# Two of eight K-tile pairs of ten up strips by Strassen's seven products, with the inner activations kept whole until the down stage

## What is computed

```python
def swiglu(x, w_up, w_down):
    g, u = jnp.split(x @ w_up, 2, axis=-1)      # w_up 2048 x 11264, w_down 5632 x 2048
    return (jax.nn.silu(g) * u) @ w_down

def reference(x, ...):
    h = x
    for l in range(DEPTH):                      # DEPTH = 1
        h = h + 0.5 * rms_norm(swiglu(rms_norm(h, ffn1_pre[l]), ffn1_up[l], ffn1_down[l]), ffn1_post[l])
        mix = hybrid_mixer(rms_norm(h, mix_pre[l]), ...)
        h = h + rms_norm(mix, mix_post[l])
        h = h + 0.5 * rms_norm(swiglu(rms_norm(h, ffn2_pre[l]), ffn2_up[l], ffn2_down[l]), ffn2_post[l])
    return h
```

## Time and profile before

| | |
|---|---|
| median of 3 runs | 2430.61 us (2430.49 to 2430.75) |
| profiled execution, its own time | 2430.32 us |
| its span in the trace | 2428.5 us |
| granted TensorE clock, mean | 0.999 |
| TensorE busy | 2412.1 us, 10823 matmuls |
| VectorE busy | 1293.1 us, 1395 instructions |
| ScalarE busy | 1155.4 us, 1340 instructions |
| GpSimd busy | 213.7 us, 400 instructions |
| up stages | 22 strips, 20 of them (2 to 11 of each block) touched by the change |

### The profile page before, as it was taken

The page is one execution under the profiler, slowest core; times in us unless marked ns, Lnnn a source line. Parts: engine busy times, 40 slices in busy tenths (PEclk is TensorE's granted clock), DMA queues, the critical chain, the costliest instruction groups (busy, mean ns, idle before and its releaser), DMA issues.

```text
span 2428.5 us, 32988 instructions
## 1 busy us (share of the span) xinstructions
PE 2412.1 (99%) x10823; PEld 1986.7 (82%) x10823; DVE 1293.1 (53%) x1395; ACT 1155.4 (48%) x1340; POOL 213.7 (9%) x400
## 2 busy tenths in 40 slices
PE   9999999999999999999999999999999999999998
PEld 7888888888887788887888888888888888888887
DVE  5555555554547555555545554555655555555444
ACT  6454544543445454454544444444554554544443
POOL 1212112110001000000000000000211212111000
PEclk9999999999999999999999999999999999999999
DMA  8767667665656555565656666655666666666664
GB/s 257 212 202 205 203 206 209 202 203 191 195 186 184 156 173 175 164 186 159 199 184 200 193 194 191 194 182 175 197 212 203 210 201 196 209 207 199 192 195 158
DMA packets 265725, 470.91 MB, mean 194 GB/s; under 512 B 21056, under 2 KB 54512, under 8 KB 265296
## 3 DMA queue, kind: packets, MB, share of 16 engines
q1 hardware_dynamic: 252752, 453.04, 60.5%
q0 software_dynamic: 12752, 17.24, 2.3%
q10 hardware_dynamic: 176, 0.07, 0.0%
HBM read 456.64 MB, written 2.10 MB: 189 GB/s over the span
## 4 chain that ended last, share of the span: by engine, by line
PE 98%; DVE 1%; ACT 1%; issue 0%; DMA 0%; ACTq 0%; DVEq 0%; SPq 0%; POOL 0%; POOLq 0%
PE acc L580 32%; PE acc L582 32%; PE acc L581 32%; PE bank L601 1%; PE bank L824 0%; PE bank L764 0%; PE bank L790 0%; DVE xT_lo L1232 0%; DVE w_lo L1221 0%; PE bank L845 0%; DVE h L1283 0%; ACT w_hi L923 0%; DMA h<-in_x_dram 0%; ACT xT_hi L945 0%; PE bank L811 0%
## 5 line engine op out<-in xcount | busy, mean ns | idle before, releaser
L1221 DVE TENSOR_TENSOR w_lo<-w_raw,w_hi 128x1024 fp32r<-128x1024 f32 x856 | 1048.3, 1227 | 1041.0 <-ACT w_hi L923 1033.1
L923 ACT ACTIVATE w_hi<-w_raw 128x1024 fp32r<-128x1024 f32 x856 | 906.3, 1061 | 1170.8 <-PE acc L582 1163.6
L580 PE MATMUL acc<-w_hi,xT_hi 128*128 128x512 f32 x2464 | 967.2, 393 | 6.1 <-DVE xT_lo L1232 3.9
L582 PE MATMUL acc<-w_hi,xT_lo 128*128 128x512 f32 x2464 | 959.9, 390 | 0.0
L581 PE MATMUL acc<-w_lo,xT_hi 128*128 128x512 f32 x2464 | 959.5, 389 | 0.0
L580 PEld LDWEIGHTS acc<-w_hi,xT_hi 128*128 128x128 f32 x2464 | 463.0, 188 | 105.6 <-issue 5.0
L582 PEld LDWEIGHTS acc<-w_hi,xT_lo 128*128 128x128 f32 x2464 | 462.8, 188 | 97.1
L581 PEld LDWEIGHTS acc<-w_lo,xT_hi 128*128 128x128 f32 x2464 | 463.1, 188 | 95.5 <-issue 1.0
L580 PE MATMUL acc<-w_hi,act_hi 128*128 128x512 f32 x704 | 273.9, 389 | 0.0
L582 PE MATMUL acc<-w_hi,act_lo 128*128 128x512 f32 x704 | 273.9, 389 | 0.0
L581 PE MATMUL acc<-w_lo,act_hi 128*128 128x512 f32 x704 | 273.9, 389 | 0.0
(11 more groups left out here) (145 smaller groups left out, 973.7 us busy)
## 6 DMA issues: line engine op xcount, KB each, us to landing
w_raw<-in_ffn_up_dram SPq DMA_DIRECT2D x352, 512.0 KB, 4.3
w_raw<-in_ffn_down_dram SPq DMA_DIRECT2D x176, 512.0 KB, 4.5
w_raw<-in_w_gate_dram SPq DMA_DIRECT2D x96, 512.0 KB, 4.1
w_raw<-in_w_in_dram SPq DMA_DIRECT2D x72, 512.0 KB, 3.6
w_raw<-in_w_in_dram SPq DMA_DIRECT2D x128, 256.0 KB, 3.0
w_raw<-in_w_ret_out_dram SPq DMA_DIRECT2D x32, 512.0 KB, 4.7
w_raw<-in_w_out_dram SPq DMA_DIRECT2D x32, 512.0 KB, 4.4
hid_T<-blocks POOLq DMA_DIRECT2D x352, 32.0 KB, 3.4
```

The lines of the kernel that those rows point to most:

```text
L580: pe.matmul(pair[m][:, :], xh, wh, start=(first and kk == 0), stop=False)
L582: mm = pe.matmul(pair[m][:, :], xl, wh, start=False, stop=(last and kk == KG - 1))
L923: act.activation(w_hi[:, s, :], w_raw[:, s, :], ACT.Copy).then_inc(w_rounded, 1)
L1221: dve.tensor_tensor(w_lo[:, s, :], w_raw[:, s, :], w_hi[:, s, :].bitcast(f32), ALU.subtract).then_inc(w_split, 1)
```

## The change

Strip 1 of each block stays as it was, in a section of its own (`first0`, `first1`) and no longer under Ifs; the loop runs over strips 2 to 11. There six of the eight K-tile pairs are multiplied as before, and pairs 6 and 7 each by Strassen's scheme in Winograd's form: the two K-tiles, the two row tiles and the gate and upper columns make a 2 by 2 by 2 block product of eight products, which becomes seven, of three matmuls each. Two products take plain blocks, one the input sum S4 with a weight block, three the sums S by T, and one a plain input with T4. They go into four scratch banks (`bank0` to `bank3`) and the accumulators, and VectorE puts them together (`u2` to `u5`) before Silu, which now reads SBUF. Row tile 1 has another RMS scale than row tile 0; `h_scaled` takes its input over to the scale of tile 0, and `to_tile1` takes the sums back.

Each pair needs four weight sums on VectorE (`t_raw`: one add over 1024 columns, two over 512), split like the weights (`t_hi`, `t_lo`). The upper group of such a pair is split only in its second half.

```diff
+QUADS = ((4, 5, 6), (10, 11, 7))
+PLAIN_GATE = ((0, 0), (1, 1), (2, 2), (3, 3), (6, 4), (7, 5))
+PLAIN_UP = ((8, 0), (9, 1), (12, 2), (13, 3), (14, 4), (15, 5))
+        T_AT = {ng - 3 + pair: (j, pair) for j, (ng, nu, k) in enumerate(QUADS) for pair in range(2)}
# sync, ahead of the load of groups 8, 9, 14, 15
+                            sp.wait_ge(t_summed, 3 * (quad(f, i, QUAD_GATE[n - SLOTS]) + 1))
# gpsimd
-            pool.dma_start(post_gain[:, :], on_all(t["ffn1_post"][0], D)).then_inc(gain_landed, 16)
             pool.wait_ge(setup_done, 1)
...
             rsqrt("pre0", rs_pre[:, 0, :])
-            with pool.Fori(0, NUP) as i:
-                turn_hidden(0, i)
+            with pool.Fori(0, NUP) as p:
+                turn_hidden(0, p)
+            wait_strip_read(pool, "up0", NST - 1, 1)
+            pool.dma_start(post_gain[:, :], on_all(t["ffn1_post"][0], D)).then_inc(gain_landed, 16)
             residual(0)
# tensor
+                p1 = three(bank[0][:, :], *x(0), *w(ng, 0), first, last)
+                three(gate[0][:, :], *x(1), *w(ng, 1), False, last).then_inc(w_used, 1)
+                pe.wait_ge(w_split, group(sec, i, nu) + 1 + SLOTS)
+                three(upper[0][:, :], *s(3), *w(nu, 1), first, False).then_inc(w_used, 1)
+                pe.wait_ge(t_split, 2 * quad(f, i, j) + 1)
+                p7 = three(bank[3][:, :], *s(2), *tt(1), first, last)
+                p5 = three(bank[1][:, :], *s(0), *tt(0), first, last)
+                pe.wait_ge(t_split, 2 * quad(f, i, j) + 2)
+                p6 = three(bank[2][:, :], *s(1), *tt(2), first, last)
+                three(gate[1][:, :], *a22, *tt(3), False, last).then_inc(t_used, 1)
...
+                    if n == 11:
+                        scaled_transposes(f)
+                pe.wait_ge(s_split, f + 1)
+                with pe.Fori(0, NST) as i:
...
-                            pe.wait_ge(hid_split, turns(f, NUP - 2))
-                        if n == GF - 2:
-                            pe.wait_ge(hid_split, turns(f, NUP - 1))
+                        if n < GF and n % 2 == 0:
+                            pe.wait_ge(hid_split, turns(f, n // 2))
# scalar: hidden_hi; vector: hidden_lo in the same places
+                        if n in (14, 15):
+                            with act.If(i > NST - 2):
+                                hidden_hi(f, n - 14)
...
+                        if n % 2 == 0 and n // 2 + 2 < NUP:
+                            with act.If(i < 1):
+                                hidden_hi(f, n // 2 + 2)
# vector, strip 1
+                    if n == 12:
+                        input_sums(f)
+                    if n == 14:
+                        dve.wait_ge(s_rounded, f + 1)
+                        dve.tensor_tensor(s_lo..., s_raw..., s_hi..., ALU.subtract).then_inc(s_split, 1)
# vector, strips 2 to 11
+                        if n + SLOTS in QUAD_GATE:
+                            sum13(f, i, QUAD_GATE[n + SLOTS])
                         rest_group(sec, i, n)
+                        if n + SLOTS in QUAD_GATE:
+                            sum24(f, i, QUAD_GATE[n + SLOTS])
```

More of the change, by code:

```diff
@@ L91, in bank_uses, with strassen @@
     use("gains", 3)
+    def strassen(f):
+        use(f"s{f}", 2, 3)
+        for _ in range(NST):
+            use(f"p{f}", 0, 1, 2, 3)
     transposed("x0")
+    strassen(0)
     transposed("x1")
@@ L668, in tail, with three @@
                 tile_by_tile(product, range(total - SLOTS, total), {(1, SLOTS - 2): pieces})
-            def swiglu(f):
[L671 to L685, removed]
+            def three(dst, xh, xl, wh, wl, start, stop):
+                pe.matmul(dst, xh, wh, start=start, stop=False)
+                pe.matmul(dst, xh, wl, start=False, stop=False)
+                return pe.matmul(dst, xl, wh, start=False, stop=stop)
@@ L1005, in output_strips @@
                     round_group(sec, i, n)
-                    if hook is not None and n == SLOTS + 1:
-                        hook()
+                    if hook is not None:
+                        hook(n)
                 def tile0():
@@ L1028, in swiglu @@
             def swiglu(f):
+                sec = f"first{f}"
+                for n in range(2 * GD):
+                    round_group(sec, 0, n)
+                    if f == 0 and n in (0, 2):
+                        x_hi(n // 2 + 2)
+                    if n == (3 if f == 0 else 2):
+                        if f == 0:
+                            for c in range(CH):
+                                act.wait_ge(x_landed[c], 16)
+                        input_squares(2 * f)
+                    if n == GD - 1:
+                        wait_strip(act, sec, 0, n)
+                        act.wait_ge(rs_ready, MEAN[f"pre{2 * f}"] + 1)
+                        pair = pair_of(sec, 0)
+                        for m in range(MT):
+                            last = act.activation(gate_sb[:, m, :], acc[pair][m][:, :], ACT.Silu,
+                                                  scale=rs_pre[:, 2 * f, m:m + 1])
+                        last.then_inc(acc_read[pair], 1)
+                    if n == 13:
+                        act.wait_ge(s_summed, f + 1)
+                        act.activation(s_hi[:, :, :, :].rearrange("p a b n -> p (a b n)"),
+                                       s_raw[:, :, :, :].rearrange("p a b n -> p (a b n)"), ACT.Copy).then_inc(s_rounded, 1)
@@ L1367, in swiglu @@
+                    last.then_inc(combined, 1)
+                    wait_combined(dve, f, i, "hid")
+                    turn_blocks()
                 if f == 0:
```

386 lines of the change are left out of this document (299 added, 87 removed).

## The result

The changed kernel takes 2445.7 us (median of 4 runs, 2443.9 to 2447.4) against 2430.55 us before (2430.43 to 2430.75). The ratio is 1.0061, 95% interval 1.0049 to 1.0073: it is slower by 15.1 us, 0.6%. The forecast was 2444.0, the range 2436 to 2462. The profiled execution took 2447.4 us, its span 2445.6.

The account below looks back on a forecast made before the run. TensorE, busy 99% of the span, was taken as the bound, so matmul count and late operands decide. -27.2 + 1.8 + 7.8 + 0.8 - 1.0 + 31.2 = +13.4 us gave 2444.0 us, range 2436 to 2462.

Parts of the forecast that it names:

- Matmuls, -27.2: Up strips: 3 fewer matmuls a pair, two pairs a strip, 20 strips, 120 x 0.2267 us: -27.2 us.
- The rival in which the seven products save nothing: Up strips: matmuls into eight banks in turn stand further apart, so nothing is saved; 2471 us, chance 0.03.
- The run, +1.8: VectorE's work from strip end to first seven products ends at S + 14.21, making TensorE 0.1 us late in 18 strips.
- The rival with the longer run: VectorE instructions start only at the previous record's end; run 0.9 us longer, 16 us more, 2460 us; chance 0.18.
- Strip 1, +7.8: Strip 1 to strip 2: input sums make TensorE 2.2 us late, 2.3 with restart, plus 1.6 clock, in each block.
- Transposes, +0.8: Four transposes of `h_scaled` cost 0.4 us in each block: +0.8 us.
- the table load, -1.0: Second block's start: ScalarE's 1.28 us table load ahead of three roundings goes, and TensorE's wait with it: -1.0 us.
- Into the down stage, +31.2: Group 4, first down strip: VectorE waits for the late post_gain copy; TensorE stands 13.9 us, 15.6 with restart and clock, per block.
- the clock behind this stretch: After the idleness entering the down stage, TensorE runs at the lower clock for a while: 1.6 us lost in each block.
- The clock did not hold: Rival that the clock holds behind the four idle stretches: 4 x 1.6 us less, 2437.6 us; chance 0.13.
- The wait for `post_gain` cost its full price: Down stage: rival that this wait costs nothing, making the kernel faster at 2415 us; chance 0.04.

Follow-up runs that it names:

- third edit: Changed kernel with VectorE's post_gain wait at its first reader, input sums two to three groups earlier, first two activation splits at groups 13 and 14: 2404.85 us.
- the split order: Against the kernel with all three edits, VectorE splits T2 and T4 of the first pair before group 6's weights in each up strip: 2403.5 us.
- the copy alone: Kernel before, without Strassen's products; GpSimd issues the post_gain copy of blocks 1 and 3 behind the turns of the hidden strips: 2453.9 us.
- the sums early: Changed kernel with the preparation of strip 1's input sums two to three groups earlier on all engines: 2437.3 us.
- the late wait: Changed kernel with VectorE's wait for post_gain moved from ahead of its down loop to group 15, just ahead of the first reader: 2414.5 us.

## Why the prediction was right

The sum was +13.4 us, and the medians differ by 15.1. Taking the idle stretches away one after the other leads from the changed kernel down to 27.0 us under the kernel before, and so prices the terms: down stage 32.5 (31.2 and the third edit's 1.3) for 31.2, strip 1 8.4 for 7.8, the run 1.3 for 1.8, the rest -27.0 for -27.4. Term by term:

**Matmuls, -27.2.** Shown. The period of a strip is that of 186 matmuls plus 0.11. With all new waits taken away (the split order) the kernel is 27.0 us under the one before, where -27.2 + 0.8 - 1.0 = -27.4 was due. The rival in which the seven products save nothing is out.

**The run, +1.8.** Shown in its reason, and in its size as 1.3 to 1.9. Its end was forecast at S + 14.21 and lies at 14.21; 18 waits, 0.2 us each at the weight load, 0.1 at the matmul. The rival with the longer run would have had it 0.9 us later: VectorE's record of 1.23 us at 443.72 is followed by the next start 1.14 later, before the record's end. In this run only those instructions start behind the record's end that read what the one before them wrote, such as the one at 446.31, 0.11 behind the end of the record at 445.46. The rule that I had named beside that rival is half of what the Trainium skill says there: "VectorE: DVE Perf Modes", The DRAIN you can't avoid, goes on that a next operation that is not held starts earlier. The rows agree with that, and not with the rule taken by itself.

**Strip 1, +7.8.** Both waits came, of 2.39 and 2.49 us in the view and so 2.55 and 2.65 by start distances, where I had 2.2. Taking them away gave 8.4; less these 5.2, that leaves 1.6 of clock and restart each, for 1.7.

**Transposes, +0.8, and the table load, -1.0.** The four transposes again stand 0.36 us ahead of the next matmul (46.32, 46.68). At the start of the second block the three roundings now begin with no table load ahead of them, and the wait of 0.76 is gone.

**Into the down stage, +31.2.** This is the whole loss, and here the total hides errors that cancel. The times from TensorE's group 0, forecast and measured in block 1: turn ended 7.9 and 7.8; the sixteen copies 7.82 and 8.67 long; `post_gain` issued at 16.3 and 17.3; VectorE on again at 22.2 and 22.5; TensorE at 24.8 and 25.1. The copies took 0.85 more than the earlier trace rows and the landing about as much less than the 5.9 I took from the earlier trace rows; that these two cancel is luck. The 0.85 is not a matter of load: in the changed kernel the loop counter picks the place in `act_raw`, and its turns take 8.67 us. In the run with the copy ahead of the last turn, that turn stands behind the loop with a fixed place and takes 7.90; those in the loop take 8.67 there too. These are all three copies of `post_gain` in the changed kernel:

```profile
DMA to landing us min/median/max: 4.9/5.0/6.0
```

The estimate by the Trainium skill ("DMA: Bandwidth & Descriptors", Anatomy of one DMA), 4.4 us, is nearer to these than to the earlier trace rows, and still under the shortest.

The term that was mis-sized is the clock behind this stretch. Removing the two waits gave 31.2 us, and by start distances they are 25.7; 5.5 are left, about 2.8 a block for the 1.7 of clock and restart that I had put there from a stretch of 1.91 us. The rows of the changed kernel have 2.7 and 2.3 (last section). The 1.07 at group 0 comes on top, and its removal gave 1.3 for both blocks: in all 32.5 for 31.2. That is most of the 1.7 us by which the forecast was low.

**Slips in the working.** The upper end of this term, 39 with a landing of 9.5, should be 38.4, and the upper ends of the terms add up to 2458 us, not to 2456. The 1.15 that I set beside the 1.91 for the earlier trace rows is a distance between starts; as idleness it is the 0.76 of the row. Neither moves the forecast.

**The rivals.** The clock did not hold behind the long stretches. The wait for `post_gain` cost its full price, and the run with the copy alone in the kernel before shows that this step needs nothing else of the change.

## What to carry over

When a buffer is lent to another use and its old content is loaded again afterwards, follow that load through its queue and through the wait of its reader: here the lending saved memory and the reload, behind sixteen small copies and with its wait ahead of unrelated work, cost more than 120 matmuls gave. Put a wait directly ahead of the first instruction that needs it; one line of that kind was worth 31 us. For an engine that serves deadlines, add up the run of work ahead of each deadline from start distances, not its share of busy time: VectorE at 35 of 42 us had no room at one place, and took 0.6 us more there at no cost after two of its instructions had changed places.

## What the runs showed of the hardware

**The clock after a short idleness falls in some executions and not in others, and after a long one it fell each time.** Long are six stretches of 9 to 12.7 us, two each in the changed kernel, in the one with the sums early and in the copy alone. The end of strip 1 has the same wait, 2.4 us, in the changed kernel and in the one with the copy ahead of the last turn. In the first, the granted clock of 60 to 64 us is 0.68 (shown above); in the second

```profile
60.00:64.00 4.00, 3.91 (x17) 3.28 (x18) 3.97 (x6) 0.88 (x1) 0.00 (x0) 1.00 0.82 242
```

with 17 matmuls in place of 11. In the kernel before a wait of 1.91 was followed by 0.57; behind the same wait the profiled execution of the changed kernel kept 1.00. In the run with the late wait it fell behind strip 1 of the first block (0.68) and not behind that of the second, in one execution. I had put the same 1.6 us behind each stretch; where it fell, the loss was 1.4 to 1.7, but it is no constant. Whether this is why the changed kernel's runs spread over 3.5 us is not shown: the runs with the late wait have both waits of strip 1 and spread over 0.15, those with the sums early have neither, though both long ones, and spread over 2.8.

**Behind the long waits the loss was 2.0 to 2.8 us, and not larger behind the longer one.** After 9.1 us (the copy alone) and after 12.7 the clock was at the lower level at the restart and for some 4 to 5.7 us more. The rows of the copy alone, first block:

```profile
504.00:508.00 4.00, 0.00 (x0) 0.00 (x0) 0.00 (x0) 0.12 (x1) 2.13 (x5) 0.95 0.45 121
508.00:512.00 4.00, 0.00 (x0) 0.00 (x0) 1.11 (x1) 0.00 (x0) 0.00 (x0) 0.50 0.44 182
512.00:516.00 4.00, 3.83 (x9) 3.06 (x10) 3.52 (x4) 0.00 (x0) 0.00 (x0) 0.50 0.54 147
```

The loss can be read from the starts of the first matmuls behind the wait. In the changed kernel the 14th starts at 515.50, and in the copy alone at 517.88:

```profile
515.50 0.39 PE L674 MATMUL acc<-w_lo,act_hi 128*128 128x512 f32 x1
```
```profile
517.88 0.40 PE L581 MATMUL acc<-w_lo,act_hi 128*128 128x512 f32 x1
```

These are 5.66 us behind 509.84 and 5.71 behind 512.17, where 13 distances of 0.2267 are 2.95: 2.7 and 2.8 us lost, restart included. Counted in the same way, the second blocks lost 2.3 and 2.0, and the two stretches of the run with the sums early 2.5 and 2.7. The times of the runs agree: 31.2 - 25.7 leaves 2.8 a block behind the longer wait, and 23.4 less two waits of 9.2 by start distances leaves 2.5 behind the shorter. Between waits of 2.5 and of 9 us nothing was measured.
